# Row-tiled state products, k steps woven into the heads, raw logits beside the output projection, norms by quarters, peeled experts

## What is computed

```python
h = _rmsnorm(x, n1) * (1.0 + sc1) + sh1
z = h @ w_in                       # hq hf hi hg gq gk gv gr gg ma mb
...
o_h, s_h_new = _gated_linear_recurrence(q_h, k_h, v_h, lg_h, s_h)
o_g, s_g_new = _gated_linear_recurrence(q_g, k_g, v_g, lg_g, s_g)
...
merged = jax.nn.sigmoid(ma) * (o_h @ w_bh) + jax.nn.sigmoid(mb) * (o_g @ w_bg)
x = x + gt1 * (merged @ w_out)
h2 = _rmsnorm(x, n2) * (1.0 + sc2) + sh2
x = x + gt2 * _moe(h2, r_w, r_b, w_gu, b_gu, w_dn, b_dn)   # router: h2 @ r_w + r_b
...
y = _rmsnorm(x, final_g)
```

## Time and profile before

| | |
|---|---|
| median of three runs | 1472.11 us (1468.68 to 1473.1) |
| the profiled execution | 1469.54 us, span 1467.5 us |
| PE busy | 1311.6 us (89%) |
| VectorE / ScalarE / GpSimd busy | 518.3 / 274.4 / 35.1 us |
| mean granted TensorE clock | 0.939 |
| HBM read | 465.66 MB |

### The profile page before, as it was taken

The page is one execution under the profiler, slowest core; times in us unless marked ns, Lnnn a source line. Parts: engine busy times, 40 slices in busy tenths (PEclk is TensorE's granted clock), DMA queues, the critical chain, the costliest instruction groups (busy, mean ns, idle before and its releaser), DMA issues.

```text
span 1467.5 us, 29078 instructions
## 1 busy us (share of the span) xinstructions
PE 1311.6 (89%) x11811; PEld 595.9 (41%) x11812; DVE 518.3 (35%) x1159; ACT 274.4 (19%) x517; POOL 35.1 (2%) x50
## 2 busy tenths in 40 slices
PE   4999999999978997978787999897999779899996
PEld 1656576666743332323132333232333223243332
DVE  4143334233483332323133344231433223243436
ACT  2130013000011221211011222121222112122222
POOL 0000000000000000000000000000000000000003
PEclk8999999989988999989798999998999989899997
DMA  9877341305275999999999999999799999998830
GB/s 388 311 304 304 113 165 58 117 17 190 83 286 228 409 412 412 416 419 418 419 416 418 418 418 417 416 419 418 283 401 409 411 416 419 418 419 355 328 129 36
DMA packets 87450, 470.92 MB, mean 321 GB/s; under 512 B 7984, under 2 KB 8000, under 8 KB 51360
## 3 DMA queue, kind: packets, MB, share of 16 engines
q1 hardware_dynamic: 84416, 460.68, 77.2%
q0 software_dynamic: 2432, 7.75, 1.9%
q10 hardware_dynamic: 576, 2.11, 0.4%
HBM read 465.66 MB, written 4.85 MB: 321 GB/s over the span
## 4 chain that ended last, share of the span: by engine, by line
PE 72%; DMA 17%; SPq 5%; DVE 3%; issue 2%; ACT 1%; DVEq 0%
PE bank L927 21%; DMA ring<-in_exp_w_dn 12%; PE bank L656 12%; PE bank L944 11%; SPq L451 4%; PE bank L896 4%; PE bank L882 4%; PE bank L793 2%; PE bank L823 2%; PE bank L654 2%; PE bank L903 2%; DMA arena<-in_exp_w_gu 2%; DMA ring<-in_ada_w 2%; DMA ring<-in_exp_w_gu 2%; ACT arena L1178 1%
## 5 line engine op out<-in xcount | busy, mean ns | idle before, releaser
L927 PE MATMUL bank<-arena 128*32 128x512 f32 x1984 | 249.2, 640 | 46.2 <-DMA arena<-in_exp_w_gu 46.0
L944 PE MATMUL bank<-ring,arena 128*32 128x256 f32 x3584 | 219.3, 382 | 33.1 <-ACT arena L1178 18.6
L1621 DVE TENSOR_SCALAR arena<-bank 128x256 f32<-128x256 f32 x56 | 23.8, 425 | 569.2 <-PE bank L927 569.2
L927 PE MATMUL bank<-ring,arena 128*32 128x512 f32 x1600 | 190.8, 622 | 19.0 <-DMA ring<-in_exp_w_gu 19.0
L1615 DVE TENSOR_TENSOR gates<-gates,bank 128x1280 f32<-128x1280 f32 x112 | 166.7, 1488 | 92.7 <-PE bank L896 92.7
L656 PE MATMUL bank<-arena,ring 128*128 128x320 f32 (+1 forms) x592 | 177.4, 461 | 2.7 <-DVE arena L1253 2.0
L944 PEld LDWEIGHTS bank<-ring,arena 128*32 128x32 f32 x3584 | 105.5, 109 | 131.1 <-issue 54.0
L656 PEld LDWEIGHTS bank<-arena,ring 128*128 128x128 f32 (+1 forms) x592 | 117.3, 201 | 66.6 <-issue 25.1
L927 PEld LDWEIGHTS bank<-arena 128*32 128x32 f32 x1984 | 56.3, 112 | 214.3 <-DMA arena<-in_exp_w_gu 106.5
L1175 ACT ACTIVATE arena<-arena 128x256 f32<-128x256 f32 x56 | 23.4, 417 | 459.1 <-DVE arena L1621 459.1
L927 PEld LDWEIGHTS bank<-ring,arena 128*32 128x32 f32 x1600 | 48.3, 112 | 141.8 <-issue 97.7
(11 more groups left out here) (259 smaller groups left out, 926.1 us busy)
## 6 DMA issues: line engine op xcount, KB each, us to landing
ring<-in_exp_w_gu SPq DMA_DIRECT2D x128, 1024.0 KB, 20.2
ring<-in_exp_w_dn SPq DMA_DIRECT2D x128, 1024.0 KB, 11.0
arena<-in_exp_w_gu SPq DMA_DIRECT2D x128, 1024.0 KB, 19.5
ring<-in_ada_w SPq DMA_DIRECT2D x24, 1024.0 KB, 21.1
ring<-in_w_in SPq DMA_DIRECT2D x20, 1024.0 KB, 10.2
ring<-in_w_out SPq DMA_DIRECT2D x4, 1024.0 KB, 7.3
ring<-in_w_in SPq DMA_DIRECT2D x4, 528.0 KB, 10.3
arena<-in_state_hgrn POOLq DMA_DIRECT2D x4, 512.0 KB, 7.8
```

The costliest lines, as they stand in the source:

```text
L927: last = mm(out[part(g), :, :], h2g[:, chunk(k)], w[:, :, columns(g)], start=False, stop=(k == DC - 1), tile_position=(0, CAP * g))
L944: last = mm(banks[2][part(g), HALF:2 * HALF], actT[:, chunk(k)], pair(item_slot(DC + k // 2))[:, k % 2, columns(g)], start=(k == 0), stop= ...
```

## The change

- **State products:** the mask holds two chunks instead of four (`vmask`, `chunk`), and each product is cut into two row tiles of 64 rows with 256 columns, the upper rows' chunks into one bank and the lower rows' into the other; `chunk_state` finds a chunk again.
- **Weaving:** `z_block` becomes a generator, `z_steps`, one step per k. Two steps come ahead of each attention product, and one at each of six places inside a head's products; what is left of the block follows them. Four ma blocks move from between the recurrences into the GLA heads, and the second head of each GLA pair gets a block. The HGRN norms are spread, and the GLA heads start, after ma3.
- **Logits:** VectorE multiplies each updated feature chunk by its gain at once; the router's product runs on these raw values beside the output blocks, the shift's share of the logits is a product of its own (`lsh`), and the token's norm is multiplied in later.
- **Norms by quarters:** the sums of squares come out as four quarters of 80 tokens on four groups of partitions, so that root and reciprocal work on 80 columns; four products spread them back over the partitions, and the following steps read them from PSUM. ScalarE adds the shift.
- **Experts:** PE's first five registers are loaded ahead of the position table, and the first four experts' loops stand ahead of the loop over groups.
- **End:** GpSimd's share goes to VectorE.

```diff
-        (4, "u"): ["mb0"], (4, "b"): ["mb1"], (4, "c0"): ["mb2"],
-        (5, "u"): ["mb3"], (5, "b"): ["mb4"], (5, "c0"): ["mb5"]}
+        (4, "a"): ["ma4"], (4, "u"): ["ma5"], (4, "b"): ["ma6"], (4, "c0"): ["ma7"], (4, "c1"): ["mb0"],
+        (5, "a"): ["mb1"], (5, "u"): ["mb2"], (5, "b"): ["mb3"], (5, "c0"): ["mb4"], (5, "c1"): ["mb5"]}
...
-    out += [(n, o, bank) for (n, o), bank in zip(owned(blocks(4)[:6]), (5, 6, 0, 1, 2, 3))]
-    out += [(f"nrm{n}", "v", (4, 0, 1, 2)[n]) for n in range(4)]
-    out += [(n, o, bank) for (n, o), bank in zip(owned(blocks(4)[6:]), (5, 6))]
+    out += [(n, o, bank) for (n, o), bank in zip(owned(blocks(4)[:4]), (5, 6, 0, 1))]
+    out += [(f"nrm{n}", "v", (2, 3, 4, 0)[n]) for n in range(4)]
...
+
+        def chunk_state(c):
+            at = (c // 4 * 2 + c % 2) * P
+            return banks[3 + c % 4 // 2][:, at:at + P]
...
-                if x < 3:
-                    sp.wait_ge(y_ready, x + 1)
-                else:
-                    sp.wait_ge(y_by_pool, 1)
+                sp.wait_ge(y_ready, x + 1)
...
-            wait_taken(pool, TURN["place"])
-            count = pool.value_load(itemtab[0:1, E:E + 1], min_val=E, max_val=NI - 1)
...
-            def z_block(name):
+            def z_steps(name):
...
-            def fill(ui, place):
+            def filling(ui, place):
                 for name in FILL.get((ui, place), []):
-                    z_block(name)
+                    yield from z_steps(name)
+
+            def some(blocks, n=1):
+                for _ in range(n):
+                    next(blocks, None)
+
+            def all_of(blocks):
+                for _ in blocks:
+                    pass
 
             group(0)
             ada(1)
@@ -701,14 +703,16 @@
                     for p, (t0, tn) in enumerate(TILES):
                         last = nc.tensor.transpose(bKD[0:tn, p * P:(p + 1) * P], o["kd"][:, u, t0:t0 + tn], ident)
                     last.then_inc(kd_flipped, 1)
+                    wide = filling(ui, "a")
                     for (_, _, hh, n, p0, dk) in heads:
+                        some(wide, 2)
...
-                    fill(ui, "a")
+                    all_of(wide)
...
                         for p in range(2):
-                            last = mm(bU[p][p0:p0 + dk, :], kdtok[:, p, p0:p0 + dk],
-                                      vmask[bi][p].rearrange("p c v -> p (c v)"), start=True, stop=True)
+                            for x in range(2):
+                                last = mm(bU[x][p0:p0 + dk, p * 2 * P:(p + 1) * 2 * P], kdtok[64 * x:64 * x + 64, p, p0:p0 + dk],
+                                          vmask[bi][p][64 * x:64 * x + 64, :, :].rearrange("p c v -> p (c v)"),
+                                          start=True, stop=True, tile_position=(64 * x, p0))
                         last.then_inc(u_ready, 1)
                         if hh == 0:
-                            fill(ui, "u")
-                    fill(ui, "b")
+                            all_of(filling(ui, "u"))
...
+                        wide = filling(ui, f"c{hh}")
...
+                        some(wide)
...
+                            if c in (3, 6):
+                                some(wide)
...
+                            if s in (1, 4):
+                                some(wide)
+                        some(wide)
...
-                        fill(ui, f"c{hh}")
+                        all_of(wide)
...
-            for f in range(2, 6):
+            for f in range(2, 4):
                 z_block(f"ma{f}")
             spread_norms(0)
-            for f in range(6, DC):
-                z_block(f"ma{f}")
-            wait_rec_banks(TURN["mb0"])
+            wait_rec_banks(TURN["ma4"])
             recurrence(1)
...
+                pe.wait_ge(u_scaled, f + 1)
+                ins = mm(banks[7][0:E, 0:T], rw[:, f, :], hT[:, f, :], start=(f == 0), stop=(f == DC - 1))
+                if f == DC - 1:
+                    ins.then_inc(turn_filled, 1)
+
+            def quarter_sums(b, src, start, stop):
+                for g in range(4):
+                    ins = mm(b[CH * g:CH * g + CH, 0:QT], ones[:, 0:CH], src[:, g * QT:(g + 1) * QT], start=start, stop=stop,
+                             tile_position=(0, CH * g))
+                return ins
...
+                if f == 3:
+                    pe.wait_ge(router_landed, 32)
+                    b = open_turn("lsh")
+                    for k in range(DC):
+                        mm(b[0:NROW, 0:E], modT[:, 24 + k, :], rw[:, k, :], start=(k == 0), stop=False)
+                    mm(b[0:NROW, 0:E], ones[0:1, 0:NROW], rb, start=False, stop=True).then_inc(turn_filled, 1)
+                    for n in range(3):
+                        raw_logits(n)
+                elif f > 3:
+                    raw_logits(f - 1)
+            raw_logits(DC - 1)
             b = open_turn("ss2")
-            pe.wait_ge(x2sq_summed, 1)
-            mm(b[:, 0:T], ones[:, :], hT[:, 0, :], start=True, stop=False)
+            pe.wait_ge(x2sq_added, DC - 2)
+            quarter_sums(b, sq[0], True, False)
             pe.wait_ge(x2sq_ready, DC)
-            mm(b[:, 0:T], ones[:, :], hT[:, DC - 1, :], start=False, stop=True).then_inc(turn_filled, 1)
-
-
-            pe.wait_ge(router_landed, 32)
-            b = open_turn("logits")
-            for k in range(DC):
-                if k % 2 == 0:
-                    pe.wait_ge(h2_ready, 1 + k // 2)
-                last = mm(b[0:E, 0:T], rw[:, k, :], hT[:, k, :], start=(k == 0), stop=(k == DC - 1))
+            quarter_sums(b, sq[(DC - 1) % 2 + 1], False, True).then_inc(turn_filled, 1)
+            wait_taken(pe, TURN["logits"])
+            pe.wait_ge(r4_ready, 1)
+            for g in range(4):
+                b = open_turn(f"spread{g}")
+                mm(b[:, 0:QT], ident[CH * g:CH * g + CH, CH * g:CH * g + 1].broadcast_to([CH, P]), r4[CH * g:CH * g + CH, :],
+                   start=True, stop=True, tile_position=(CH * g, 0)).then_inc(turn_filled, 1)
...
+            for p, (t0, tn) in enumerate(TILES):
+                last = mm(b[0:tn, p * E:(p + 1) * E], logT[:, t0:t0 + tn], ident[0:E, 0:E], start=False, stop=True,
...
+            for q in range(2):
+                for p, (t0, tn) in enumerate(TILES):
                     b = open_turn(f"tok{p}{q}")
                     for j in range(4):
+                        if p == 0:
+                            pe.wait_ge(h2_ready, 4 * q + j + 1)
+                            pe.wait_ge(h2_samples, 4 * q + j + 1)
...
+            wait_taken(pe, TURN["place"])
+            _, first = nc.values_load_multi_w_load_instructions(itemtab[0:1, 0:5], engines=[mybir.EngineType.PE],
+                                                                min_val=0, max_val=NI - 1)
             pe.wait_ge(comb_ready, 1)
...
-            with pe.Fori(0, E // 4) as fours:
+            for x in range(4):
+                with pe.Fori(first[x], first[x + 1]) as i:
+                    item(i, x // 2, x % 2)
+            with pe.Fori(1, E // 4) as fours:
...
-                last = mm(banks[SCATTER[0]][:, 0:T], ones[:, :], hT[:, FEATURES[n], :], start=(n == 0), stop=(n == 7))
+                last = quarter_sums(banks[SCATTER[0]], hT[:, FEATURES[n], :], n == 0, n == 7)
             last.then_inc(ss3_ready, 1)
+            pe.wait_ge(r4_ready, 2)
+            for g in range(4):
+                last = mm(lower[:, g, 0:QT], ident[CH * g:CH * g + CH, CH * g:CH * g + 1].broadcast_to([CH, P]),
+                          r4[CH * g:CH * g + CH, :], start=True, stop=True, tile_position=(CH * g, 0))
+            last.then_inc(scale3_ready, 1)
...
-                A(hT[:, f, :], xT[:, f, :], ACT.Square, scale=ROOT_SCALE).then_inc(x2sq_ready, 1)
+                if f >= 3:
+                    act.wait_ge(x2sq_added, f - 2)
+                A(sq[f % 2 + 1 if f else 0], xT[:, f, :], ACT.Square, scale=ROOT_SCALE).then_inc(x2sq_ready, 1)
+                if f == 4:
+                    wait_filled(act, "lsh")
+                    A(lsh, bank_of("lsh")[0:NROW, 0:E], ACT.Copy).then_inc(taken["s"], 1)
+            wait_filled(act, "logits")
+            A(logT, bank_of("logits")[0:E, 0:T], ACT.Copy).then_inc(taken["s"], 1)
             wait_filled(act, "ss2")
-            A(small[:, 0:T], bank_of("ss2")[:, 0:T], ACT.Sqrt, bias=C("eps")).then_inc(taken["s"], 1)
+            A(r4, bank_of("ss2")[:, 0:QT], ACT.Sqrt, bias=C("eps")).then_inc(taken["s"], 1)
+            for f in range(DC):
+                act.wait_ge(h2_scaled, f // 2 + 1)
+                A(hT[:, f, 0:TP], hT[:, f, 0:TP], ACT.Identity, bias=modT[:, 24 + f, 0:1]).then_inc(h2_ready, 1)
             act.wait_ge(rexp_wanted, 1)
             A(comb, comb, ACT.Exp).then_inc(rexp_ready, 1)
...
-            A(small[:, 0:T], banks[SCATTER[0]][:, 0:T], ACT.Sqrt, bias=C("eps")).then_inc(root3_ready, 1)
+            A(r4, banks[SCATTER[0]][:, 0:QT], ACT.Sqrt, bias=C("eps")).then_inc(root3_ready, 1)
...
```

(50 more changed lines are left out.)

101 lines of the change are left out of this document (47 added, 54 removed).

## The result

The changed kernel took 1463.99 us, the median of seven runs from 1455.92 to 1468.31; the kernel before took 1472.11 in runs beside them. The ratio is 0.994 (95% interval 0.992 to 0.997), a gain of 8 us where 25 were forecast. Twelve later runs gave the same: 1465.35 us, ratio 0.996 (0.993 to 0.998). The profiled run is the shortest of the seven: span 1454.0 us, against 1467.5.

A forecast was written before the change was run, and what follows sets the result against it. PE bounds both recurrences; DMA and PE alternate in the experts, whose weight stream starts with PE's first item. Terms -5.4 -15.5 +0.4 -2.0 +0 -2.1 = -24.6 gave 1444.9 us profiled, 1447 us as median; range 1438 to 1461 us.

The forecast's parts named there:

- the 17.3 us of falls: Recurrences: cost of half-clock stretches in seven of eight heads; the forecast took 15.5 us of it as gained.
- 1. State products: Heads' state products in both recurrences: four half-row products overlap, saving 0.7 us a head over 8 heads, -5.4 us.
- 2. The clock: Both recurrences: k steps woven among short products make nearly all half-clock falls vanish in seven heads, -15.5 us.
- Rival A: Recurrences: the clock falls in woven heads too, above all GLA; clock term 0 to -5, 1456 to 1463 us; chance 0.14.
- Weaving costs nothing by itself: Woven heads: k steps are moved, not added; one weight load hidden, another exposed; changed rows at most 2.5 us.
- rival C: Woven heads: each insertion costs a drain and weight load; decides from 0.49 us each, 1482 us at 0.7; chance 0.05.
- 3. Between the recurrences: HGRN to GLA: wait for VectorE's norms +1.7 us, two attention mask waits vanish -1.3, together +0.4 us.
- the 1.5 us more: Between the recurrences: some +1.5 us extra if the new idle time drops the clock.
- 4. Output projection to routing: First output product to routing's first copy: 49.0 us instead of 51.0, -2.0 us, bounds +1 and -5.
- 5. Peel: Ahead of the first expert: 2.4 us register load moves from behind the position chain into it, 0, bounds -0.5 and +0.5.
- 6. The end: Kernel's end: GpSimd's share to VectorE, shorter root and reciprocal, one output transfer, -2.1 us, bounds -0.5 and -3.2.
- Rival B: Experts: weights arrive as late as now, so only the tail's gain is left, 1465 to 1472 us; chance 0.05.

The follow-up runs named there:

- experiment 1: The changed kernel run again unchanged, with a second and third profile: median 1465.35 us, ratio 0.996 to the kernel before; third profile's run 1464.37 us.
- experiment 5: State products on 128 rows and 512 columns again, against the changed kernel with `low` products moved behind the sample products: 1462.01 us, ratio 0.996 to the kernel before.
- experiment 9: Changed kernel, `low` products behind sample products, no peel, 12 steps per GLA head: 1449.79 us at six places, 1448.04 at three; variant with 8, then 16 steps: 1450.94.
- experiment 2: Changed kernel with GLA heads not woven, their blocks computed whole again, HGRN heads still woven: 1464.42 us, ratio 0.996 to the kernel before.
- experiment 3: Changed kernel with the last HGRN head's `low` products back behind the sample products, all else woven: 1458.66 us, ratio 0.992 to the kernel before.

## Why the prediction was wrong

The sign was right; the time, 1464 instead of 1447, was above the range. For the profiled execution the steps add up like this: -24.6 forecast; -1.8 for the last of the 17.3 us of falls, which went too; +5.5 for weaving in the GLA heads; +4.5 in the last HGRN head; +2.7 between routing and experts; +1.6 in the experts; -1.8 at the end; -0.2 up to the routing. That is -14.1, measured -13.5. This execution is the shortest of its seven: in the other two profiles half clock in the GLA recurrence comes on top, with 14.6 and 11.2 us. On the mean of the three profiles that is +8.6, and the last HGRN head +3.5 instead of +4.5: -6.5, where the medians gave -8.1 and, in experiment 1, -5.7 (1465.35 against 1471.06). So of the 17 us missed in the median about half is the clock in the GLA heads, a third the price of weaving there.

**1. State products: right.** Forecast -5.4 (0.7 a head for 8 heads would be -5.6), -5 to -6 by experiment 5. Row halves run beside each other: the same 1024 columns take 1.01 to 1.07 us in four products and, at full clock, took 1.71 to 1.91 in two.

**2. The clock: right for the HGRN heads, wrong for the GLA heads. This is the step that failed.** The three whole-block HGRN heads went from 37.6 to 31.3 us (value products to sum of squares, added up), and their falls vanished in all 13 profiles with a whole block woven. For the GLA heads the prediction reasoned that no stretch would be left that holds short products alone, and that the falls would then vanish. They came back in 18 of 36 heads although a step stood after every few products. Weaving is not a matter of yes or no: with the same eight steps the HGRN heads held and the GLA heads did not, with four the HGRN heads fell, with twelve the GLA heads held. Rival A named this, and even the heads; it was given 0.14 and taken as nearly all or nothing, 1456 to 1463 us. What the runs don't settle is why the GLA heads need more steps: their products have half the rows, but no run changed the rows alone. The Trainium skill, "TensorE: Matmul & The Clock Gate", Part 1, calls the number of slow products at a kernel's start "run-variable". No run here bears on the start; the three profiles of the changed kernel, with falls in zero, three and two GLA heads, vary in the midst of steady work.

**"Weaving costs nothing by itself": wrong by 5.5 us.** The bound took the chunk products alone for the price of a change (1.75 against 1.70; seven products, which show as 14 instructions). Rows with a step between 64-row products on both sides did not exist before, but both changes did, and more of their price stands in the group ahead of the change:

```profile
262.78 1.93 PE L719 MATMUL bank<-arena 128*64 128x512 f32 x4
...
275.42 0.78 PE L732 MATMUL bank<-arena,vtok 128*128 128x128 f32 x6
```

Ahead of 64-row products the value products take 276.13 - 275.42 = 0.71 us, in an HGRN head 214.37 - 213.75 = 0.62. Ahead of 128-row products the 64-row attention products take 262.78 - 261.89 = 0.89 us, in an HGRN head, without a change, 0.80. With the 0.05 that makes 0.23 us a place, and 5.5 us for the 24 places of the GLA heads. Measured were 0.27 us a place in experiment 9 and 1.4/6 = 0.23 in experiment 2, each for two changes; still below the 0.49 from which rival C decides. In the HGRN heads, where all products have 128 rows, six places cost 0.1 us a head (9.58 against 0.61 + 1.54 + 1.86 + 1.06 + 4.41 = 9.48). The Trainium skill, "TensorEngine Tiling (Array Packing)", Key Properties, says that changing the tiling mode drains TensorE; the trace agrees in that a place which is entered and left costs 0.27 us, though no row shows what TensorE does in it.

**3. Between the recurrences: the wait right (1.75, forecast 1.7), the last HGRN head wrong.** The two waits for the attention mask vanished as forecast, and the 1.5 us more "if this idle time drops the clock" came in two profiles (1.6 us, experiments 1 and 9). For the last HGRN head the prediction left the stretch as it was, "still only the two tiny `low` products". But the change weaves these as well. In the first profile half clock begins at 208.9, ahead of the sequences, and lasts twice as long: 4.5 us, 2.2 to 4.5 in the four profiles with the `low` products woven. Some 1 us of it is VectorE, whose work they had covered (1.81 instead of 0.74 us of waiting); experiment 3 gives it back.

**4. Output projection to routing: right.** 48.83 us, forecast 49.0, and 48.8 to 49.1 in all 15 profiles since; the steps on the way lie within 1.0 us of the forecast ones. What was not priced is what lies behind: in this execution the token transpositions fall into a half-clock stretch (410.3 to 420.5) and take 5.42 us, and the rank products start 4.8 instead of 3.4 us behind the copy.

**5. Peel: forecast 0 ± 0.5, some +2 where the chain could have run at full clock, 0 where not.** The load's time moved as forecast. Not seen was that part of it had lain beside VectorE's last copies, and that the chain behind it would run wholly or in part at half clock, as it did in all ten profiles with the peel.

**6. The end: -2.1 forecast, -3.9 measured** (22.20 to 18.25 us from the last scattering products to the end). The last square came 1.2 us earlier, not 0.3. And the quarter sums gained 0.65, not nothing: before, the sums ended at half clock 0.65 us behind the table load. The rest, 2.1 us, was priced at 1.8.

**Rival B fell:** from the first expert to the last scattering products it took 997.7 to 1000.9 us in all 15 profiles since, 999.3 before. A us gained ahead of the experts is a us of the kernel.

One slip changes nothing: the chances counted as "faster" (0.61, 0.03, 0.14 and 0.12) already add up to 0.90 without a part of B, not to 0.89.
